# A hybrid decoder layer on one core: the beginning rebuilt (own buffers for the embedding weights, p on a second queue in three parts, warm-up matmuls, first norm in two halves)

## The reference

```python
h = rmsnorm(x, ln_pre)
z = h @ w_in                       # 8 groups of columns, 58 tiles of 128
ya = conformer_conv(c_val, c_glu, ...)          # GLU, 31 taps, LayerNorm, swish, product
ya = (ya * silu(c_gate)) @ w_br_conv
yb = sliding_window_sink_attention(q, k, v, sinks, positions)
yb = (yb * silu(a_gate)) @ w_br_attn
m = sigmoid(g_conv) * ya + sigmoid(g_attn) * yb
x = x + rmsnorm(m @ w_out, ln_post)
x = x + sigmoid(x @ w_ple_gate) * (p @ w_ple_proj)     # p: 1024 x 256
```

## Time and profile before

| | before |
|---|---|
| median of 3 runs | 1201.85 us (1201.72 to 1203.98) |
| the profiled execution's own time | 1201.38 us |
| its span, first to last instruction | 1199.6 us |
| TensorE busy | 1183.9 us |
| VectorE busy | 825.6 us |
| ScalarE busy | 393.5 us |
| mean granted TensorE clock | 0.998 |

### The profile page before, as it was taken

How to read it: one execution, slowest core, us unless ns; L and a number is a source line. 1 busy time by engine, 2 the same in 40 slices (tenths; PEclk the granted TensorE clock), 3 DMA queues, 4 the chain that set the end, 5 groups by cost and what they waited for, 6 DMA issues and landing times.

```text
span 1199.6 us, 14489 instructions
## 1 busy us (share of the span) xinstructions
PE 1183.9 (99%) x5496; PEld 961.4 (80%) x5496; DVE 825.6 (69%) x895; ACT 393.5 (33%) x676; POOL 17.9 (1%) x16
## 2 busy tenths in 40 slices
PE   7999999999999999999999999999999999999998
PEld 6788888888888888777777788888888888888886
DVE  5899999999999883577676485674332444457565
ACT  6422211221121111376766342331221221344331
POOL 1011000000000000000000000000000000000000
PEclk9999999999999999999999999999999999999999
DMA  9321122122221224212121111223223222334734
GB/s 341 118 97 67 56 87 70 56 84 70 70 88 70 79 58 100 48 54 71 36 71 36 53 53 52 81 95 105 96 79 105 106 81 94 126 113 147 262 106 175
DMA packets 33748, 112.63 MB, mean 94 GB/s; under 512 B 4432, under 2 KB 5136, under 8 KB 33456
## 3 DMA queue, kind: packets, MB, share of 16 engines
q1 hardware_dynamic: 23056, 74.42, 19.1%
q10 hardware_dynamic: 10656, 37.75, 8.9%
HBM read 87.91 MB, written 20.97 MB: 91 GB/s over the span
## 4 chain that ended last, share of the span: by engine, by line
PE 96%; DVE 2%; DMA 1%; SPq 0%; ACT 0%; issue 0%; ACTq 0%; DVEq 0%
PE psg L391 79%; PE psg L613 7%; PE psb L550 2%; PE psg L409 2%; PE psg L580 1%; PE psg L565 1%; PE psg L585 1%; DVE sums L1095 1%; PE psg L438 1%; DMA conv<-xT 1%; PE psb L471 0%; PE psb L462 0%; DVE conv L1111 0%; PE psb L491 0%; DVE w_lo L1054 0%
## 5 line engine op out<-in xcount | busy, mean ns | idle before, releaser
L391 PE MATMUL psg<-h_hi,w_hi 128*128 128x512 f32 x768 | 237.9, 391 | 0.0
L391 PE MATMUL psg<-h_lo,w_hi 128*128 128x512 f32 x768 | 236.5, 389 | 0.0
L391 PE MATMUL psg<-h_hi,w_lo 128*128 128x512 f32 x768 | 236.5, 389 | 0.0
L700 ACT ACTIVATE w_hi<-w_raw 128x1024 fp32r<-128x1024 f32 x112 | 118.4, 1057 | 224.9 <-PE psg L391 210.7
L1054 DVE TENSOR_TENSOR w_lo<-w_raw,w_hi 128x1024 fp32r<-128x1024 f32 x115 | 140.5, 1221 | 73.7 <-ACT w_hi L700 73.2
L391 PEld LDWEIGHTS psg<-h_hi,w_hi 128*128 128x128 f32 x768 | 143.7, 188 | 31.1 <-issue 1.7
L391 PEld LDWEIGHTS psg<-h_lo,w_hi 128*128 128x128 f32 x768 | 144.1, 188 | 30.1
L391 PEld LDWEIGHTS psg<-h_hi,w_lo 128*128 128x128 f32 x768 | 144.1, 188 | 30.0
L1170 DVE SCALAR_TENSOR_TENSOR conv<-u,cols,conv 128x1024 f32<-128x1024 f32 x120 | 154.0, 1283 | 0.0
L1170 DVE SCALAR_TENSOR_TENSOR work<-u,cols,work 128x1024 f32<-128x1024 f32 x112 | 145.5, 1299 | 0.0
L613 PE MATMUL psg<-h_hi,w_hi 128*128 128x512 f32 x128 | 55.3, 432 | 0.0
(11 more groups left out here) (187 smaller groups left out, 1757.2 us busy)
## 6 DMA issues: line engine op xcount, KB each, us to landing
w_raw<-weights SPq DMA_DIRECT2D x115, 512.0 KB, 3.4
gates<-ring ACTq DMA_DIRECT2D x24, 512.0 KB, 2.6
ring<-gates ACTq DMA_DIRECT2D x24, 512.0 KB, 3.5
conv<-xT SPq DMA_DIRECT2D x8, 512.0 KB, 9.7
ple<-ple_out ACTq DMA_DIRECT2D x8, 512.0 KB, 5.7
x_ring<-xT ACTq DMA_DIRECT2D x16, 256.0 KB, 3.4
ple_all<-ple ACTq DMA_DIRECT2D x2, 2048.0 KB, 12.9
outT<-result SPq DMA_DIRECT2D x16, 256.0 KB, 3.8
```

The costliest lines, as they stand in the source:

```text
L391: mm = nc.tensor.matmul(psg[:, slot, h * HALF:(h + 1) * HALF], w[:, wslot, (wk + k) * P:(wk + k + 1) * P], r[:, k, h * HALF:(h + 1) * HALF ...
L700: nc.scalar.activation(w_hi[:, j % 2, :], w_raw[:, j % 2, :], ACT.Copy).then_inc(w_hi_ready, 1)
```

## The change

It touches the beginning, up to the first pair of tiles; what comes behind is renumbered but otherwise the same.

- The embedding weights have buffers of their own (`wp_raw`, `wp_hi`, `wp_lo`), so the ring's two slots are loaded with tiles 0 and 1 at once, behind the constants. ACT rounds the second step, not DVE.
- p is loaded from ACT's queue in three parts: block 0 in two halves of 512 columns, block 1 whole. ACT rounds and DVE subtracts in the same three parts.
- TensorE runs eight fp32 matmuls of ones by ones (128 columns) before the first tile.
- Embedding tile 7 goes to `psb` banks 2 and 3. DVE copies tile 1 out; ACT the others. All spills are issued by SP, behind the loads, with weight tiles 2 and 3 between the sixth and the seventh.
- The square of block 0 is written into `sums` directly, so DVE adds seven times and doesn't copy.
- The first norm is done in two column halves: mean square after tile 5, both halves; the broadcast of the first half in the middle of tile 6, that of the second half after tile 6.
- DVE makes the low parts of weight tiles 0 and 1 after the diagonals and before it scales x. Its small work on the constants moves behind that.

The core of the diff (what only renumbers is left out):

```diff
-            return (0, 1, None, 0, 1, None, 0, 1)[t]
+            return (0, 1, None, 0, 1, None, 0, None)[t]
+        P_PARTS = ((0, slice(0, HALF)), (0, slice(HALF, S)), (1, slice(0, S)))
...
-            sp.dma_start(w_raw[:, 0, 0:FIRST], WALL[:, 0, 0:FIRST]).then_inc(w_first_loaded, 16)
-            for k in range(PLE_KT):
-                sp.dma_start(p_raw[:, k, :], PT[:, k, :]).then_inc(p_loaded[k], 16)
-            sp.dma_start(w_raw[:, 0, FIRST:], WALL[:, 0, FIRST:]).then_inc(w_loaded[0], 16)
+            sp.dma_start(wp_raw[:, 0, 0:FIRST], WALL[:, 0, 0:FIRST]).then_inc(w_first_loaded, 16)
+            sp.dma_start(wp_raw[:, 0, FIRST:], WALL[:, 0, FIRST:]).then_inc(wp_loaded[0], 16)
             for k in range(4):
                 sp.dma_start(conv[:, k, :], XT[:, k, :]).then_inc(x_loaded[k], 16)
-            load_weights(1, 1)
+            sp.dma_start(wp_raw[:, 1, :], WALL[:, 1, :]).then_inc(wp_loaded[1], 16)
             for k in range(4, KT):
                 sp.dma_start(conv[:, k, :], XT[:, k, :]).then_inc(x_loaded[k], 16)
...
+            load_weights(PLE_STEPS, 0)
+            load_weights(PLE_STEPS + 1, 1)
...
+            for t in range(6):
+                spill_ple(t)
+            load_weights(PLE_STEPS + 2, 0, PLE_STEPS + 1)
+            load_weights(PLE_STEPS + 3, 1, PLE_STEPS + 2)
+            spill_ple(6)
+            spill_ple(7)
...
             pe.wait_ge(init_done, 1)
+            for n in range(8):
+                nc.tensor.matmul(psb[:, 0, 0:P], ones[:], ones[:], start=True, stop=True)
             pe.wait_ge(w_first_hi, 1)
             ple_tile(0)
...
             ple_tile(4)
-            mean_square(sq_used, KT, bank=0)
             pe.wait_ge(ple_free, 1)
             ple_tile(5)
+            mean_square(sq_used, KT, range(NB // 2), 0)
+            mean_square(sq_used, KT, range(NB // 2, NB), 1)
             pe.wait_ge(ps_free[0], 2)
-            ple_tile(6)
-            pe.wait_ge(ps_free[1], 2)
+            ple_step(6, 0)
+            broadcast(1, (0,))
+            ple_step(6, 1)
+            broadcast(2, (1,), first=1)
+            pe.wait_ge(ple_free, 2)
             ple_tile(7)
...
+            for n, (k, part) in enumerate(P_PARTS):
+                act.dma_start(p_raw[:, k, part], PT[:, k, part]).then_inc(p_loaded[n], 16)
             act.wait_ge(w_first_loaded, 16)
...
+            for n, (k, part) in enumerate(P_PARTS):
+                act.wait_ge(p_loaded[n], 16)
+                nc.scalar.activation(p_hi[:, k, part], p_raw[:, k, part], ACT.Copy).then_inc(p_hi_ready, 1)
...
+            square_x(0)
+            square_x(1)
+            read_ple(0)
+            square_x(2)
+            square_x(3)
+            act.wait_ge(wp_loaded[1], 16)
+            nc.scalar.activation(wp_hi[:, 1, :], wp_raw[:, 1, :], ACT.Copy).then_inc(w_hi_ready, 1)
+            square_x(4)
+            read_ple(2)
+            square_x(5)
+            square_x(6)
+            square_x(7)
+            read_ple(3)
+            first_high(0)
+            read_ple(4)
+            first_high(1)
+            read_ple(5)
             h_high(0)
-            h_high(1)
             read_ple(6)
...
             dve.wait_ge(consts_loaded, 16 * 2)
+            variance(1, first, 0)
+            variance(2, second, 1)
+            diagonal(1, first)
+            diagonal(2, second, at=NB // 2)
+            tile_low(0)
+            tile_low(1)
+            dve.wait_ge(bcast_done, 2)
```

More of the change, by code:

```diff
@@ L441, in late_pair, with norm_pair @@
                         mm.then_inc(tile_done, 1)
-            def norm_pair(first, rhs_hi, rhs_lo, ready, half, n):
-                blocks = (range(NB // 2), range(NB // 2, NB))[n - 3]
+            def norm_pair(first, rhs_hi, rhs_lo, ready, half, h):
+                blocks = (range(NB // 2), range(NB // 2, NB))[h]
                 def sum_squares(k):
                     if k == 4:
-                        mean_square(sq_used, (n - 1) * KT, blocks)
+                        mean_square(sq_used, (h + 2) * KT, blocks)
                 def roots(k):
                     if k == 1:
-                        broadcast(n, (n - 3,))
+                        broadcast(h + 4, (h,))
                 tile(first // 2, 0, rhs_hi, rhs_lo, ready, (half,), sum_squares)
@@ L472, in broadcast, with ple_step @@
                 mm.then_inc(bcast_done, 1)
+            def ple_step(t, k):
+                slot = ple_slot(t)
+                cols_k = slice(((t % 4) * PLE_KT + k) * P, ((t % 4) * PLE_KT + k + 1) * P)
+                for n, (w, r) in enumerate(((wp_hi, p_hi), (wp_lo, p_hi), (wp_hi, p_lo))):
+                    if t == 0 and n == 1 and k == 0:
+                        pe.wait_ge(w_first_lo, 1)
+                    for h in range(2):
+                        if t == 0 and n == 0:
+                            pe.wait_ge(p_hi_ready, 3 if k == 1 else h + 1)
+                        if t == 0 and n == 2:
+                            pe.wait_ge(p_lo_ready, 3 if k == 1 else h + 1)
+                        out = psb[:, 2 + h, :] if slot is None else psg[:, slot, h * HALF:(h + 1) * HALF]
+                        mm = nc.tensor.matmul(out, w[:, t // 4, cols_k], r[:, k, h * HALF:(h + 1) * HALF],
+                                              start=(k == 0 and n == 0), stop=(k == PLE_KT - 1 and n == 2))
+                if k == PLE_KT - 1:
+                    mm.then_inc(tile_done, 1)
@@ L475, in ple_tile @@
             def ple_tile(t):
-                slot = ple_slot(t)
                 for k in range(PLE_KT):
[L479 to L492, removed]
@@ L644, in _ @@
             tile(D0 // 2 + 3, 0, h_hi, h_lo, beside=lambda k: mean_square(var_summed, KT + 1) if k == 1 else None)
-            tile(D0 // 2 + 3, 1, h_hi, h_lo, beside=lambda k: broadcast(2, source=diag_ln) if k == 1 else None)
+            tile(D0 // 2 + 3, 1, h_hi, h_lo, beside=lambda k: broadcast(3, source=diag_ln) if k == 1 else None)
             pairs(E0, F0, o_hi, o_lo, KT)
@@ L1096, in _ @@
+            nc.vector.tensor_copy(ple_out[:, 1, :], psg[:, 1, :]).then_inc(ps_free[1], 1)
+            for k in range(1, KT):
+                dve.wait_ge(sq_ready, k)
+                dve.wait_ge(sq_used, k)
+                nc.vector.tensor_tensor(sums[:], sums[:], (tanh_t, work)[k % 2][:], ALU.add).then_inc(sq_used, 1)
                 if k == 3:
-                    dve.wait_ge(w_loaded[1], 16)
-                    nc.vector.tensor_copy(w_hi[:, 1, :], w_raw[:, 1, :]).then_inc(w_hi_ready, 1)
@@ L1330, in _ @@
                 if m == 6:
-                    variance(2)
-                    diagonal(2, into=diag_ln)
+                    variance(3)
+                    diagonal(3, into=diag_ln)
                 dve.wait_ge(tanh_ready, m + (2 * KT + 1))
@@ L1444, in _ @@
                 if m == 0:
-                    variance(3, slice(0, NB // 2))
-                    diagonal(3, slice(0, NB // 2))
+                    variance(4, slice(0, NB // 2))
+                    diagonal(4, slice(0, NB // 2))
                 some_x1(0, m)
```

140 lines of the change are left out of this document (61 added, 79 removed).

## The result

The changed kernel takes 1206.87 us (median of 6 runs, 1206.06 to 1208.24), against 1202.75 us (1201.71 to 1203.98) for the kernel before beside it: a ratio of 1.0036, 95% interval 1.0026 to 1.0046. The forecast was 1202.8 with a range of 1199.9 to 1205.2, so it was wrong, on the slow side. The profiled execution of the changed kernel took 1208.05, its span is 1206.3 us, 6.7 more than that of the kernel before.

A forecast was written before the change was run, and what follows sets the result against it. TensorE bounds the kernel, busy 1183.9 of 1199.6 us. Third step of tile 0 at L + 32.7, 41.7 against 40.71, is +1.0: 1201.38 becomes 1202.4, plus 0.47 for the median, said as 1202.8, range 1199.9 to 1205.2.

The forecast's parts named there:

- the point to follow: Start of the third step of tile 0, after the norm: from 40.71 to 41.7 us, each microsecond counting in the end.
- A: Rival at the loads: p's last part lands at 7.9, 1201.7 us, or even 6.65, 1200.5 us; chance 0.25.
- C: Rival at the start: ACT's table load holds back its DMA issues; +4.5 us, 1206.3 us; chance 0.06.
- L: The time at which p's last part lands, between 7.9 and 9.3 us, taken as 9.0.
- p's landing: Arrival of p's last part from ACT's queue, interleaved with x: 9.0 us against 6.65 in the kernel before.
- Tile 1 at L + 3.4: Embedding tile 1 starts 3.4 us after p's last part lands, for rounding and low parts: 12.4 against 11.25.
- rival B: Clock falls back during waits ahead of tile 1: 0.6 to 1.9 us on top, 1203.4 to 1204.7; chance 0.25.
- the warm-ups: Eight matmuls before the first tile, ending between 4.9 and 7.7 us: cost 0, gain only if the clock stays up.
- Free: First mean-square half to diagonal: 2.1 to 2.35 us, covered by 2.34 of TensorE's work, so no cost.
- The norm: Tile 1 to third step of tile 0: 20.25 + 0.2 + 8.85 us; the part after the broadcast gains 1.1.
- Spills and loads on SP's queue: Eight spills behind the loads, weight tiles 2 and 3 coming at about 29 us: cost 0.
- D: Rival in the attention: shifted start changes the clock's fall after its wait, up to 1.7 us either way; chance 0.08.

The follow-up runs named there:

- e5: Changed kernel with p in two whole blocks on SP's queue, not three parts on ACT's: 1203.26 us, ratio 1.0005 to the kernel before.
- e7: e6 without the eight warm-up matmuls: 1202.49 us, ratio 0.9995 to the kernel before.
- e9: Changed kernel with p in two whole blocks, not three parts, still on ACT's queue: 1203.77 us, ratio 1.0008 to the kernel before.
- e13: Changed kernel with twenty-eight warm-up matmuls, not eight: 1206.00 us, ratio 1.0026 to the kernel before.
- e10: e6 with seventeen warm-up matmuls, not eight: 1202.06 us, ratio 0.9991 to the kernel before.
- e6: e5 with embedding tile 1 copied out by ACT, not DVE: 1201.91 us, ratio 0.9992 to the kernel before.
- e2: Changed kernel without the eight warm-up matmuls: 1206.60 us, ratio 1.0027 to the kernel before.
- e3: Changed kernel with embedding tile 1 copied out by ACT, not DVE: 1205.88 us, ratio 1.0019 to the kernel before.
- e14: Changed kernel itself, measured and profiled once more: 1207.42 us, ratio 1.0035 to the kernel before.
- e8: e6 with both mean-square halves between tile 5's steps and both broadcasts before tile 6's second step: 1201.43 us, ratio 0.9988 to the kernel before.
- e12: e8 with seventeen warm-up matmuls as in e10, and ten matmuls ahead of the attention's first scores: 1202.25 us, ratio 0.9993 to the kernel before.
- e4: Kernel before with p's two blocks issued from ACT's queue, not SP's: 1203.84 us, ratio 1.0005 to the kernel before.
- e1: Changed kernel with p's three parts on SP's queue, not ACT's: 1203.58 us, ratio 1.0003 to the kernel before.

## Why the prediction was wrong

- **What bounds the kernel, and the point to follow.** Right. Of the 6.7 us in the span 5.5 had arisen by the third step of tile 0.
- **Rivals A and C.** Neither came: ACT issued p from 0.76 to 2.14 us and its table load followed at 2.17, so C's hold-up didn't occur, and A's early landing didn't either. A's price for p at 6.65 (39.35) was too good besides, since it has tile 1 at L + 3.4: with p at 7.05 to 7.5 and eight warm-ups or none (e5 to e7) tile 1 came at L + 4.4 to 5.1.
- **p's landing, taken as 9.0 with 9.3 as its late end: the step that failed first.** It was 10.7. I counted p's bytes against x's as equals, and used the rate of whole blocks. e9 shows the missing term: in turns by packet a 2 KB packet earns half of what a 4 KB one does, and all transfers together were slower by a fifth. Whole blocks land at 8.5, inside my bounds. The bound itself was drawn too narrow: it held only mixes at the old rate. In the medians this step is nearly all of the loss, as e9 is at 1.0008 of before.
- **Tile 1 at L + 3.4.** Right where the clock was up: 3.3 in e13 and e10. It was 3.9 in the changed kernel, where the clock was down.
- **The clock, given as rival B.** It came. B put 0.6 to 1.9 on it, and e13 measured 1.2 to 1.9. It should not have been a rival at 0.25: with the landing at 10.7 TensorE had three waits, and the one of 2.57 us alone is near the attention's. Even with p early, in e5 and e6, the warm-ups' clock was gone within tile 0. The prediction saw that the warm-ups are worth nothing with p late (e2). They ended at 4.45 us, before the 4.9 to 7.7 put on them.
- **DVE's copy of tile 1: left out.** I took ACT's list of work to find when the sums are ready, and asked only what DVE adds. A wait put ahead of seven additions in an ordered queue holds all of them, and ACT behind them: 0.95 us (e3, e6). The sums were ready at 30.2, not 23.8, 0.5 us before tile 5's end, where 2.2 had been put. "Free" was luck there.
- **The norm.** Tile 1 to the third step was put at 29.3 us; e6, without the wait and with the clock up from early in tile 1, has 29.32. The halves, the power (1.99 for both, 1.0 each) and the diagonals were as worked out. The moved low parts, put at 0.2, cost nothing: DVE had finished them and waited 0.22 us for TensorE's broadcast. The gain of this part is as small as it was put, 0.1 us against the 29.46 of the kernel before.
- **Spills and loads on SP's queue.** No matmul waited for them. Right, though the loads of tiles 2 and 3 were issued at 35.9 us and not at 29.
- **The attention (D).** The price, 1.7, was wrong: 1.0 where the scores are slow, else nothing, since ACT covers it. It is the part of the profiled difference that isn't in the beginning, and it isn't shown to come of the change, since e14, the same kernel, has none of it.

In sum the forecast's 1.0 us had to be 1.0 + 1.7 (landing) + 1.9 (clock, 0.5 before tile 1 and 1.4 in it) + 0.95 (copy) + 1.0 (scores), 6.6 against 6.7 in the spans. For e14 it is 1.0 + 1.7 + 1.2 + 0.95, 4.9 against 5.2. In the medians it is 4.1, since the kernel before has slower executions too: the forecast stood on a median of 1201.85, and 0.9 of its distance to 1206.87 lies in that base.

## What to carry to other kernels

In these runs a transfer on a second queue took turns by packet with the first, so what is needed first must not have the smaller rows there, and in front on the one queue it landed earliest. Warm-up matmuls only pay if they reach up to the work that they warm. And where an in-order engine is given a new wait, write down everything behind it before its time is called free.

## What was not expected of the hardware

- Halves of a block on a second queue brought the DMA engines from 1.37 MB to 1.10 MB between 3 and 7 us.
- In e8 and e12 1.95 us of one-column matmuls after a wait of 0.37 and 0.53 were followed by the lower clock (0.53 and 0.59 from 27 to 30.5 us), though TensorE counts as busy there in the page. They alone aren't the cause: in e4 the same matmuls after a wait of 0.41, and in the kernel before after 0.32, were followed by pairs 0.46 us apart. What decides stays open.
- The same wait is followed by either clock. After 2.8 us of waiting in the attention the scores took 1.16 us in e6, e7 and e14 and 2.08 in e1, e2, e3, e9 and the first profile of the changed kernel.
- The record of the granted clock isn't complete: e14 shows 1.00 from 14 to 15 us, as the kernel before does from 6.5 to 10, while pairs of matmuls start 0.85 us apart. The distance of the pairs is the surer sign.
